# State-space mixer: the rows of decay exponents spread by adding transfers from DRAM instead of by products with a selector

## The reference, cut to what matters

```python
def ssd_chunked(xs, dt, a, bm, cm, h0):
    xdt = (xs * dt[..., None]).reshape(b, nc, CHUNK, SSD_GROUPS, R, SSD_HEAD_DIM)
    a_cs = jnp.cumsum(...(dt * a)..., axis=-1)          # running log decay, per head
    lower = jnp.tril(jnp.ones((CHUNK, CHUNK), dtype=bool))
    seg = jnp.exp(jnp.where(lower, a_cs[..., :, None] - a_cs[..., None, :], -jnp.inf))
    cb = jnp.einsum('bclgn,bcsgn->bcgls', cc, bc)
    y_diag = jnp.einsum('bcgls,bcgrls,bcsgrp->bclgrp', cb, seg, xdt)
    states = jnp.einsum('bcsgn,bcgrs,bcsgrp->bcgrpn', bc, jnp.exp(a_cs[..., -1:] - a_cs), xdt)
    ...
    y_off = jnp.einsum('bclgn,cbgrpn,bcgrl->bclgrp', cc, h_prev, jnp.exp(a_cs))
    y = (y_diag + y_off).reshape(b, L, SSD_HEADS, SSD_HEAD_DIM)
```

## Time and profile before

| what | us |
|---|---|
| median of 3 runs | 1667.0 (1666.6 to 1667.98) |
| span of the profiled execution, first to last instruction | 1665.4 |
| median less span | 1.6 |
| PE busy | 1655.6 (99%) |
| DVE busy | 1229.5 (74%) |
| ACT busy | 927.8 (56%) |
| POOL busy | 148.0 (9%) |

### The profile page before, as it was taken

The page is one execution under the profiler, slowest core; times in us unless marked ns, Lnnn a source line. Parts: engine busy times, 40 slices in busy tenths (PEclk is TensorE's granted clock), DMA queues, the critical chain, the costliest instruction groups (busy, mean ns, idle before and its releaser), DMA issues.

```text
span 1665.4 us, 22804 instructions
## 1 busy us (share of the span) xinstructions
PE 1655.6 (99%) x8756; PEld 1415.4 (85%) x8756; DVE 1229.5 (74%) x1630; ACT 927.8 (56%) x1396; POOL 148.0 (9%) x210
## 2 busy tenths in 40 slices
PE   9999999999999999999999999999999999999998
PEld 7888888888888888888899888888888889988887
DVE  6888776788888777776688876655766668986564
ACT  6655577655555455545566455554645458655553
POOL 1100100000211001110010011000002012310000
PEclk9999999999999999999999999999999999999999
DMA  8977552787859876687655557554667545357551
GB/s 292 340 261 258 170 191 103 248 295 256 286 174 334 261 247 215 258 301 256 203 166 182 169 174 265 200 189 141 225 213 252 186 144 203 108 180 244 189 190 64
DMA packets 99356, 359.32 MB, mean 216 GB/s; under 512 B 11184, under 2 KB 11440, under 8 KB 99248
## 3 DMA queue, kind: packets, MB, share of 16 engines
q1 hardware_dynamic: 92736, 335.59, 59.0%
q0 software_dynamic: 6368, 22.21, 4.3%
q10 hardware_dynamic: 144, 0.07, 0.0%
HBM read 356.70 MB, written 1.12 MB: 215 GB/s over the span
## 4 chain that ended last, share of the span: by engine, by line
PE 94%; DVE 3%; DMA 2%; issue 1%; ACT 0%; SPq 0%; DVEq 0%; POOLq 0%; POOL 0%; ACTq 0%
PE dn L539 28%; PE gu L494 19%; PE gu L528 10%; PE tp L528 10%; PE gu L527 5%; PE tp L527 5%; PE dn L509 4%; DMA raw<-in_weights 2%; PE gu L524 1%; PE tp L524 1%; PE tp L457 1%; PE dn L528 1%; PE gu L525 1%; PE tp L525 1%; PE dn L494 1%; DVE w_lo L1768 1%
## 5 line engine op out<-in xcount | busy, mean ns | idle before, releaser
L1768 DVE TENSOR_TENSOR w_lo<-raw,w_hi 128x1024 fp32r<-128x1024 f32 x520 | 639.2, 1240 | 217.3 <-ACT w_hi L1135 212.4
L1135 ACT ACTIVATE w_hi<-raw 128x1024 fp32r<-128x1024 f32 x520 | 549.4, 1059 | 322.5 <-PE dn L539 147.7
L494 PE MATMUL gu<-w_hi,hT 128*128 128x512 f32 x1056 | 328.9, 393 | 1.6 <-DVE w_lo L1764 1.1
L528 PE MATMUL gu<-hT,w_hi 128*128 128x512 f32 x728 | 259.6, 396 | 0.0
L528 PE MATMUL tp<-hT,w_hi 128*128 128x512 f32 x728 | 259.5, 396 | 0.0
L539 PE MATMUL dn<-w_hi,actT_hi 128*128 128x512 f32 x608 | 238.8, 393 | 0.0
L539 PE MATMUL dn<-w_lo,actT_hi 128*128 128x512 f32 x608 | 236.9, 390 | 0.0
L539 PE MATMUL dn<-w_hi,actT_lo 128*128 128x512 f32 x608 | 236.7, 389 | 0.0
L494 PEld LDWEIGHTS gu<-w_hi,hT 128*128 128x128 f32 x1056 | 195.6, 188 | 42.6 <-DVE hT L1776 1.5
L494 PE MATMUL gu<-w_lo,hT 128*128 128x512 f32 x528 | 205.9, 390 | 0.0
L527 PE MATMUL gu<-hT,w_lo 128*128 128x256 f32 x728 | 203.1, 279 | 0.0
(11 more groups left out here) (366 smaller groups left out, 2092.3 us busy)
## 6 DMA issues: line engine op xcount, KB each, us to landing
raw<-in_weights SPq DMA_DIRECT2D x563, 512.0 KB, 4.3
arena<-in_ada_w SPq DMA_DIRECT2D x72, 512.0 KB, 4.3
post_row<-in_post_rows POOLq DMA_DIRECT2D x10, 512.0 KB, 5.6
pre_row<-in_pre_rows POOLq DMA_DIRECT2D x10, 512.0 KB, 7.2
mod_row<-mod POOLq DMA_DIRECT2D x9, 512.0 KB, 10.0
shift_row<-mod POOLq DMA_DIRECT2D x5, 512.0 KB, 9.8
x<-in_x_in SPq DMA_DIRECT2D x4, 256.0 KB, 6.0
arena<-in_c_rows POOLq DMA_DIRECT2D x2, 512.0 KB, 9.3
```

The costliest lines, as they stand in the source:

```text
L494: m = pe.matmul(bank, h[:, k, t * P:(t + 1) * P], w[:, r, kk * 512:(kk + 1) * 512], start=k == 0 and q == 0, stop=k == KT - 1 and q == 2)
L528: m = pe.matmul(o, w_hi[:, r, c], hT[:, :, k, :], start=False, stop=k == KT - 1)
L1135: act.activation(o, i, ACT.Copy, **kw).then_inc(done, 1)
L1768: dve.tensor_tensor(w_lo[:, r, :], raw[:, n % RAW, :], w_hi[:, r, :].bitcast(F32), ALU.subtract).then_inc(lo_ready, 1)
```

## The change

It has five parts.

1. The 12 rows of running sums are copied by ACT to `log_rows` in SBUF and stored by an ACT DMA to a DRAM tensor `row_store` (24 KB). POOL waits for that, and then issues six DMAs (`rows_spread`), one per pair of heads, which read two rows, spread them over 128 partitions and add them (`accum_op`) to what is in `decays`. What is there is the mask, loaded by six POOL DMAs of 512 KB in `ffn_4`, one at every third slot from slot 32 on. `decay(r)` now waits for the r-th adding transfer and works in place in SBUF. `differences` is gone, and so are the DVE operations that made the selector, the mask, the split of the rows and a zeroed wide tile.
2. `decay(r)` stands at other places among ACT's operations, each later, against the slots, than before or at the same place.
3. The `dt` slot: only its 192 numbers are loaded and split; upper and lower part stand side by side, and PE makes 16 products with 48 stationary columns instead of 24 with 24; DVE adds the two halves afterwards.
4. `far_inputs` and the products with the skip weights move from POOL to DVE; `far_scaled` is two products of 128x384 and two sums of 128x384 per group, and the PE is released after the products.
5. `state_slot(8)` goes ahead of `correlations(1)`, `state_slot(9)` ahead of `far(1)`; on DVE `weighted(1)` goes behind a slot's lower part, `both_ways(2)` and `tapped(1, 8)`.

```diff
+DT_SLOTS = (BASE["ctx_mix"], BASE["ssd"] + 8)
-        log_rows = actT_hi[:, :, :].rearrange("p d l -> p (d l)")
+        log_rows = part(12800, 2 * TOK)[0:SSD_H, :]
...
+                c = slice(0, KT * NDT if n in DT_SLOTS else SLOT)
+                sp.dma_start(raw[:, n % RAW, c], weights[bass.ts(n, P), c]).then_inc(landed[n % RAW], 16)
...
# PE, dt_slot
-                    for q, (h, w) in enumerate(((hT_hi, w_hi), (hT_lo, w_hi), (hT_hi, w_lo))):
-                        m = pe.matmul(tp[0:NDT, 0, 0:TOK], w[:, r, k * NDT:(k + 1) * NDT], h[:, k, :],
+                    for q, h in enumerate((hT_hi, hT_lo)):
+                        m = pe.matmul(tp[0:2 * NDT, 0, 0:TOK], w_hi[:, r, 2 * k * NDT:2 * (k + 1) * NDT], h[:, k, :],
...
# PE, ssd
-                def differences(r):
-                    ...
-                    for q in range(2):
-                        h, bank = 2 * r + q, rows_bank(r)[:, q, :]
-                        pe.matmul(bank, select[:, h:h + 1].broadcast_to([P, P]), log_rows, start=True, stop=False)
-                        m = pe.matmul(bank.rearrange("p (d t c) -> p d t c", d=2, t=TT), unit,
-                                      outside.unsqueeze(2).broadcast_to([P, 2, TT, P]), start=False, stop=True)
-                    m.then_inc(rows_psum, 1)
...
                 correlations(0)
                 state_slot(7)
                 far(0)
                 outputs(0)
+                state_slot(8)
                 correlations(1)
-                state_slot(8)
+                state_slot(9)
                 far(1)
                 outputs(1)
-                state_slot(9)
                 correlations(2)
...
# ACT
                 def decay(r):
-                    act.wait_ge(rows_psum, r + 1)
+                    act.wait_ge(rows_added[r], 16)
...
-                copy(log_rows, tp[:, 1, :], row_split_hi)
+                copy(log_rows, tp[0:SSD_H, 1, :], rows_taken)
+                act.wait_ge(rows_taken, 1)
+                act.dma_start(row_store, log_rows).then_inc(rows_stored, 16)
...
# DVE
+                    for t in range(TT):
+                        w = exps[:, t * NDT:(t + 1) * NDT].rearrange("p (d h) -> p d h", d=2)[:, :, heads]
+                        dve.tensor_tensor(far_parts(g)[:, t, :, :, :], gu[:, t, 0:2 * GW].rearrange("p (d j c) -> p d j c", d=2, j=HPG),
+                                          w.unsqueeze(3).broadcast_to([P, 2, HPG, SSD_P]), ALU.mult).then_inc(yoff_used, 1)
...
                     for d in range(2):
-                        for t in range(TT):
-                            for j in range(HPG):
...
+                        m = dve.tensor_tensor(acc, far_parts(g)[:, :, d, :, :], acc, ALU.add)
...
# POOL
+            def rows_spread():
+                pool.wait_ge(rows_stored, 16)
+                for r in range(PAIRS):
+                    pool.wait_ge(outside_in[r], 16)
+                    pool.dma_start(decays[:, 2 * r:2 * r + 2, :], row_store[2 * r:2 * r + 2, :].partition_broadcast(P),
+                                   accum_op=ALU.add).then_inc(rows_added[r], 16)
...
+                    for r in range(PAIRS):
+                        pool.wait_ge(slot_used, BASE[name] + 32 + 3 * r)
+                        pool.dma_start(decays[:, 2 * r:2 * r + 2, :], small["outside"].unsqueeze(1).broadcast_to([P, 2, 2 * TOK])).then_inc(outside_in[r], 16)
...
                 if name == "ssd":
+                    rows_spread()
                     later_states()
-                    far_inputs()
```

More of the change, by code:

```diff
@@ L132, with build @@
 XBC_ALL = sum(len(v) for v in XBC_UNITS)
-X_UNITS, TANH_UNITS, LOW_ROW = 3, 5, 32
+X_UNITS, TANH_UNITS = 3, 5
+PAIRS = SSD_H // 2
 MIX_AB, MIX_SC, MIX_SSD = 4, 4, 4
 MIX0 = {"ab": 0, "sc": MIX_AB, "ssd": MIX_AB + MIX_SC}
-def build(nc, weights, ada_w, x_in, ctx_in, pre_rows, post_rows, small, mod, out):
+def build(nc, weights, ada_w, x_in, ctx_in, pre_rows, post_rows, small, mod, row_store, out):
     with ExitStack() as stack:
@@ L1153, in upper @@
                         copy(w_hi[:, n % RING, c], raw[:, n % RAW, c], done, scale=pre_cols[:, k:k + 1])
+                    return
+                if n in DT_SLOTS:
+                    copy(dt_pair(n, 0), dt_raw(n), hi_ready)
                     return
@@ L1668, in ssd @@
                 after_slots(x0 + 4, 1)
-                decay(1)
+                act.wait_ge(shift_ready, 1)
+                decay(0)
                 tanh(1)
@@ L1672, in ssd @@
                 after_slots(x0 + 5, 1)
-                decay(2)
+                decay(1)
                 tanh(2)
-                decay(3)
                 centre(1, 3, s0)
@@ L1683, in ssd @@
                 tanh(4)
+                decay(2)
                 centre(1, 5, s0 + 2)
                 after_slots(s0 + 2, 1)
+                centre(1, 6, s0 + 3)
+                decay(3)
+                cb_taken(0)
+                after_slots(s0 + 3, 1)
                 decay(4)
-                centre(1, 6, s0 + 3)
-                after_slots(s0 + 3, 1)
+                copy(actT_hi[:, :, :], f_out, mix_hi)
                 decay(5)
-                cb_taken(0)
-                copy(actT_hi[:, :, :], f_out, mix_hi)
                 silu_tile(5)
@@ L2338, in weighted, with far_inputs, skipped @@
                     dve.tensor_tensor(o, o, near, ALU.mult).then_inc(g_ready, 1)
+                def far_inputs():
+                    dve.wait_ge(x_taken, TT)
+                    dve.wait_ge(state1_ready, 1)
+                    for d in range(2):
+                        w = far_rate[:, d * SSD_H:(d + 1) * SSD_H].unsqueeze(2).broadcast_to([P, SSD_H, SSD_P])
+                        dve.tensor_tensor(by_head(x_far[d]), by_head(x_tok[:, d, :]), w, ALU.mult).then_inc(far_ready, 1)
+                def skipped():
+                    for t in range(TT):
+                        w = ssd_rows[:, 2 * NDT:].unsqueeze(2).broadcast_to([P, SSD_H, SSD_P])
+                        dve.tensor_tensor(by_head(y_acc[:, t, :]), by_head(x_tok[:, t, :]), w, ALU.mult).then_inc(skip_ready, 1)
                 def far_scaled(g):
+                    heads = slice(g * HPG, (g + 1) * HPG)
                     dve.wait_ge(yoff_psum, g + 1)
@@ L2403, in ssd @@
                 gated_tiles(4)
+                far_inputs()
                 tapped(1, 5)
                 after_slots(s0 + 2, 1)
-                both_ways(2)
+                skipped()
                 tapped(1, 6)
@@ L2409, in ssd @@
                 after_slots(s0 + 3, 1)
+                both_ways(1)
                 dve.wait_ge(mix_hi, MIX0["ssd"] + 1)
@@ L2414, in ssd @@
                 y_added(0)
-                weighted(1)
+                both_ways(2)
                 after_slots(s0 + 4, 1)
                 tapped(1, 8)
+                weighted(1)
                 after_slots(s0 + 5, 1)
+                both_ways(3)
+                tapped(1, 9)
                 far_scaled(1)
-                both_ways(3)
                 y_added(1)
-                tapped(1, 9)
                 weighted(2)
@@ L2707 @@
     mod = nc.dram_tensor("mod", [ADA_N, 2, P], F32, kind="Internal").ap()
+    row_store = nc.dram_tensor("row_store", [SSD_H, 2 * TOK], F32, kind="Internal").ap()
     out = nc.dram_tensor("out", [TOK, D], F32, kind="ExternalOutput").ap()
     build(nc, aps["weights"], aps["ada_w"], aps["x_in"], aps["ctx_in"], aps["pre_rows"], aps["post_rows"],
-          {name: aps[name] for name in small_arrays}, mod, out)
+          {name: aps[name] for name in small_arrays}, mod, row_store, out)
     nc.compile()
```

116 lines of the change are left out of this document (44 added, 72 removed).

## The result

| | us |
|---|---|
| kernel before, median of 4 runs beside the changed one | 1666.8 |
| changed kernel, median of 4 runs | 1676.5 |
| ratio, with its 95% interval | 1.0056 (1.0045 to 1.0068) |
| span of the profiled execution, before and after | 1665.4 and 1674.9 |

The change makes the kernel 0.56% slower, 9.4 us (the ratio on 1666.8). The prediction said slower, by 4.1 us, and had the measured time inside its range of 1664.5 to 1683. The direction and most of the mechanism held, one term of the sum was missing. That the time lies inside the range is in part luck: it is above the 1668.5 to 1674 of the forecast case, and the range reached further up only for the adding transfers that trickle, which they did not.

What follows compares the result with a forecast made beforehand. The prediction took PE to bound the kernel, with ACT and DVE also at their limit in the mixer. On 1667.0 us: PE's work -7.3, waits +5.8, late rows +5.6, together +4.1, 1671.1 us; range 1664.5 to 1683.

Steps and rivals of the forecast that it cites:

- forecast case: Whole kernel: rows late by 3 to 9 us and no trickle, 1668.5 to 1674 us; chance 0.38.
- adding transfers that trickle: Rival, mixer: beside the weights one adding transfer ends every 5.8 us, total 1678, up to 1684; chance 0.32.
- PE's own saving, 7.3: PE's work falls by 7.3 us, 0.9 in the context stage and 6.4 in the mixer.
- d = 5.6: Lateness of the first rows at decay(0): store 3.0 plus first adding transfer 9.3 less 6.7 available; bounds 0 and 11.5.
- The extra pass for the add: First adding transfer: an add fetches two operands per result, so 1.6 us on top of 7.7.
- The five that follow keep pace: Later adding transfers land 4.3 us apart where ACT has 4.4 a step: no further wait.
- Exponentials from SBUF, 0: ACT's 48 exponentials now read SBUF: taken as 0, between -1.0 and +2.9 us.
- Waits of 1.6 + 2.8 + 1.4, and d: PE's new waits before correlations(1), outputs(1) and correlations(3), 5.8 us, plus the rows' lateness of 5.6.
- Moved work and mask loads at 0: far_inputs and skip products on DVE (3.8 us) and six mask loads in ffn_4 cost 0; uncovered, DVE's at most about 1.5.
- The cover: For DVE's moved 3.8 us: POOL stops the same work at that time, and DVE waits for ACT there anyway.
- the case of rows in time: Rival: store and first transfer stay under 6.7 us, so no lateness, 1665.5 us; chance 0.22.
- ACT and DVE keep up: Rival, mixer: rows not late and half or all of the 5.8 us of waits go, 1662.6 to 1659.7; chance 0.08.

Runs made afterwards that it cites:

- e7: Changed kernel, PE given 10 throwaway products (5, 3 and 2) ahead of its waits before x_tokens(0), correlations(1) and outputs(1); 1674.3 us, ratio 1.0040.
- e9: Changed kernel with weighted(1) on DVE directly behind y_added(0), ahead of both_ways(2), the slot's lower part and tapped(1, 8); 1674.4 us, ratio 1.0046.
- e6: Changed kernel with six plain transfers of the same size from a constant input in place of the adding ones; 1675.3 us, ratio 1.0042.
- e5: Changed kernel without its six adding transfers, the exponentials reading the tiles as the mask loads left them; 1668.2 us, ratio 1.0004.
- e8: Kernel before with dt slots of 16 products, wide far part, far inputs and skip products on DVE, rows still spread by products; 1666.5 us, ratio 0.9994.
- e4: Kernel before with one part of the change alone, dt slots of 16 products instead of 24; 1666.0 us, ratio 0.9991.
- e2: Changed kernel, PE given 36 throwaway products (21, 6 and 9) ahead of its waits before x_tokens(0), correlations(1) and outputs(1); 1691.6 us, ratio 1.0145.
- e1: Changed kernel with the adding transfers reading a constant input, so they don't wait for the stored rows; 1676.7 us, ratio 1.0048.
- e10: Changed kernel with ACT pieces moved ahead of decay(0) and decay(1), weighted(1) sooner on DVE, and both_ways(0) behind far_inputs; 1670.7 us, ratio 1.0022.

## Why the prediction was right, and where it was short

Point by point:

1. *PE's own saving, 7.3.* Right within 0.5. The dt slot saves 0.90 for 0.92, and the six pairs that are gone took 5.6 for 5.5; running sums and a Fourier piece got 0.2 longer, so the mixer saves 6.3 for 6.4. Of the context stage's 0.9, 0.4 came back there at once, as a longer wait for DVE's `hT` (0.7 instead of 0.3).
2. *d = 5.6.* The mechanism was right, its size 4.24 in the profiled execution. Store to POOL's first issue: 3.0 as taken (1394.24 to 1397.27). First landing 8.3 for 9.3, and ACT was ready 0.5 later than reckoned (1401.4 for 1400.9). This execution lies at the low end: in the traces of e7 and e9, whose edits come behind the first rows, the issue came 4.1 after the store's and ACT waited 5.74 and 5.01. The extra pass for the add, 1.6, is what was too much: e6 has no add and lands no sooner. The basis of it, the 7.7 of the earlier trace rows, was close.
3. *The five that follow keep pace.* Right. From first to last landing a step is (25.1 + 2.8 - 8.3) / 5 = 3.9 us (2.8 between the first and the last issue), for 4.3 taken and 4.4 wanted. The trickle (5.8 a step) did not come, though an adding transfer takes 2.65 us of all engines, close to the 3.1 that it was built on. The Trainium skill (Collectives: The Full Stack, the bandwidth ceiling) says for the add of a reduce-scatter that it needs two source reads and so runs at about half the rate of a copy; 2.65 against 1.29 agrees. What it slowed was the weights, 6.7 us to landing for 3.3, and the ring had the room for that. By the Trainium skill's other rule (DMA: Bandwidth & Descriptors, Anatomy of one DMA), an estimate of 3.2 us for the first of 512 KB, the rows would have been in time. But 8.3 and 8.6 were measured in this stage, so here the rule fails by a factor of more than two. The section gives the rule for transfers from GpSimd, and the store, for which the prediction used it too, goes from ACT.
4. *Exponentials from SBUF, 0.* Wrong, inside its bounds: eight take 2.35 from start to next start (1405.67 to 1408.02) where they took 1.99, 44 ns more for each and 2.1 us for 48. The Trainium skill (Perfetto Trace Analysis, Optimizing Scalar/DVE Operations) gives ScalarE about 93 ns of overhead for an access to SBUF and 51 to PSUM; 42 ns more for each fits the 44 of the trace, and would have given the term, which the rows of before (tanh and silu) left open. Whether writing over its own input has a part in it was not tried.
5. *Waits of 1.6 + 2.8 + 1.4, and d.* `silu_tile(6)` was to end at 1427.0 + d, 1431.2 with the d measured. It ended at 1435.5: 2.1 for the exponentials and 1.9 in which ACT waited for PE (0.21, 0.23 and 1.46) are most of it, and the longest of the three is for a slot that PE had worked at partly at the lower clock. For `correlations(1)` 1.6 + d was said, 5.8 with 4.2; the trace has 5.5 of it already before `x_tokens(0)`, a place that the prediction names but puts no number to, and 1.6 here. `outputs(1)`: 2.5 for 2.8, with 8.1 us on DVE as added up (1435.95 to 1444.02). `correlations(3)`: no wait for 1.4; PE had lost 3.1 us at the lower clock before it. In e5, e6, e7 and e9, where it had lost less there or nothing, 0.8 appeared.
6. *Moved work and mask loads at 0.* Right, by e8, and by PE's full 50.00 us from 1300 to 1350 beside the mask loads. The cover was the one named: the moved operations put 3.6 us on DVE, and two groups that no longer run beside POOL's work took 3.9 less (6.1 to 3.5 and 5.1 to 3.8, e4 against e8, from 1400 to 1455).

The step that failed is the sum itself. It took a wait at its own length: 11.4 us of waits were forecast and 9.6 came, so the terms that were there give +2.3 (-7.3 + 9.6). What lifts this towards the measured 9.4 (9.5 between the two spans) is the lower clock behind two of the waits, 5.6 in the trace. The last 1.6 are the 0.5 by which the waits cost more from start to start, the smaller saving (0.1 in the mixer, 0.4 in the context stage) and 0.6 that the two traces differ by before either stage begins (at the first transfer of `mod` from POOL, 410.9 and 411.5). A sign of the clock was in the trace of before, though in none of the rows above: it grants 1.00 as long as PE works, and 0.50 from 1664 to its end at 1665.4, PE's last product having ended at 1659.7. How much of the 5.6 is on the path is settled only in part. e7 takes 4.0 of it away and gains 2.7, with an interval of about 2 us on either side; in e6 some 2.3 of the second 3.1 are on the path; and the four executions of the changed kernel differ by 1.1 us where their clocks differ by about 5. That the missing term is the clock is shown, its size is not.

The rivals: e5 is the case of rows in time, and shows it at 1667.5 (by its ratio) and not 1665.5, since the terms above are missing from it as well: 1.6 of clock, and exponentials that put 2.1 more on ACT. Its 4.7 us of waits cost 5.4 from start to start. That ACT and DVE keep up is ruled out by the same run.

## To carry to other kernels

Where PE is the bound and runs without a gap, look at what else is full in the stage before taking PE's work away: here ACT had 24.68 of 25 us, its exponentials got 2.1 us longer by the change, and none of the 7.3 us came through, even with the new transfers left out (e5). Whether a better order would let some of it through there was not tried. Price a new wait of PE at its length, and as a range at the work that may follow at half the clock (2.5 us behind the wait of 5.5 here; 3.1 behind one of 2.52, and nothing behind the same one in e6). Giving PE something to do in the wait kept the clock at 1.00 (e2); the gain by it, 2.7 us in e7, is not clear of noise. And a transfer that replaces on-chip work costs twice, in its own way to landing and in what it takes from the stream of weights, so that issuing it sooner need not help (e1).

## What the hardware showed that was not expected

- The granted clock: PE stopped at 1408.9 in the changed kernel, had 1.00 from 1411 to 1412 and 0.50 from 1413 on, worked from 1414.4 and had 1.00 again from 1420. The Trainium skill (TensorE: Matmul & The Clock Gate, Part 1: The HAM clock gate) says that the array's clock is halved when PE idles, and these rows agree. But the length of one wait does not decide: 2.52 before `outputs(1)` was followed by 0.50 in the changed kernel and by 1.00 in e6. 1.64 before `correlations(1)` left the clock at 1.00 in the changed kernel and 1.79 did so in e9, while 1.9 in e5 was followed by 0.66 over five us, 1.79 in e10 by 0.50, and in e9 two of 0.59 and 0.77 close together by 0.88 and 0.78 over the two stretches of five. What decides between them was not tried.
- A product of two plain f32 tiles of 512 columns takes 0.87 us as two passes, where the row spreading products of the earlier trace rows took 0.23 each; e2 was spoilt by it.
- The first of six queued transfers from POOL lands after 8.3 us with the add (8.05 to 9.19 over six traces) and 8.6 without, though it needs 2.65 and 1.29 us of the engines. In e1, issued 6 us sooner, it landed after 5.1. What it waits for in the difference stays open.
